# A two-layer fp32 block on one core: the first weight chunk computed by passes, the modulation passes and several loads moved to later places in the stream

## What is computed (the reference, cut)

```python
def reference(x, ..., w_in, ..., c_2, ctx_2, c_ctx_2, w_mod_2, ...):
    x = first_block(x, norm_in_g, w_in, ...)      # retention + gated linear recurrence
    return second_block(x, c_2, ctx_2, ...)       # two layers, with modulation

def first_block(x, ...):
    xn = rms_norm(x, norm_in_g)                   # x: 256 tokens x 1024
    proj = xn @ w_in                              # 1024 x 6144, all fp32
    q, k, v, g_ret, x_lru, g_lru = split(proj)
    q, k = rotary(q), rotary(k) * d ** -0.5       # 8 heads of 128
    y_ret = group_norm(retention(q, k, v)) * silu(g_ret)
    y_lru = rg_lru(causal_conv(x_lru), ...) * silu(g_lru)
    return rms_norm(x + concat(y_ret, y_lru) @ w_out, norm_out_g)

def second_block(x, c, ctx, c_ctx, ...):
    for l in range(2):
        mod = silu(c) @ w_mod[l] + b_mod[l]       # 1024 x 6144, one row each
        mod_c = silu(c_ctx) @ w_mod[l] + b_mod[l]
        ...                                       # mixing branches and FFN, modulated by mod, mod_c
```

## Time and profile before

| what | us |
|---|---|
| runs without a profile: median of 3 (lowest, highest) | 1670.08 (1669.75, 1671.25) |
| the profiled execution, its own time | 1669.85 |
| its span, first to last instruction | 1668.1 |
| around the span | 1.75 |
| PE / DVE / ACT busy in the span | 1655.0 / 1237.9 / 853.8 |

### The profile page before, as it was taken

How to read it: one execution, slowest core, us unless ns; L and a number is a source line. 1 busy time by engine, 2 the same in 40 slices (tenths; PEclk the granted TensorE clock), 3 DMA queues, 4 the chain that set the end, 5 groups by cost and what they waited for, 6 DMA issues and landing times.

```text
span 1668.1 us, 25166 instructions
## 1 busy us (share of the span) xinstructions
PE 1655.0 (99%) x9776; PEld 1421.6 (85%) x9776; DVE 1237.9 (74%) x2154; ACT 853.8 (51%) x1398; POOL 0.2 (0%) x4
## 2 busy tenths in 40 slices
PE   9999999999999999999999999999999999999998
PEld 9898888778887778889888888888778999989997
DVE  7999967966787897857887775347756776677874
ACT  7676655654344443356444442347553455576653
POOL 0000000000000000000000000000000000000000
PEclk9999999999999999999999999999999999999999
DMA  8657743132235345523555556224522354545553
GB/s 343 237 203 265 247 142 104 64 127 77 69 105 187 114 146 204 201 88 133 123 189 185 187 184 222 90 76 141 113 76 76 119 162 151 190 162 174 183 204 125
DMA packets 80230, 258.02 MB, mean 155 GB/s; under 512 B 14448, under 2 KB 18800, under 8 KB 79472
## 3 DMA queue, kind: packets, MB, share of 16 engines
q1 hardware_dynamic: 74352, 248.02, 45.6%
q10 hardware_dynamic: 5760, 8.39, 1.5%
HBM read 255.31 MB, written 1.07 MB: 154 GB/s over the span
## 4 chain that ended last, share of the span: by engine, by line
PE 87%; DVE 7%; ACT 3%; issue 2%; DMA 1%; ACTq 0%; SPq 0%; DVEq 0%
PE bank L796 73%; PE bank L960 3%; PE bank L1138 2%; PE bank L1154 2%; DVE w_lo L1996 2%; PE bank L1126 2%; PE bank L1234 2%; DMA w_raw<-in_weights 1%; ACT w_hi L1345 1%; PE bank L1220 1%; DVE mod_w L2052 1%; DVE junk_gate L2052 0%; DVE ptmp L2410 0%; DVE hT_lo L2421 0%; PE bank L911 0%
## 5 line engine op out<-in xcount | busy, mean ns | idle before, releaser
L1996 DVE TENSOR_TENSOR w_lo<-w_raw,w_hi 128x1024 fp32r<-128x1024 f32 (+1 forms) x356 | 428.0, 1210 | 252.6 <-ACT w_hi L1345 251.4
L1345 ACT ACTIVATE w_hi<-w_raw 128x1024 fp32r<-128x1024 f32 (+1 forms) x356 | 370.2, 1048 | 333.1 <-PE bank L796 280.3
L796 PE MATMUL bank<-hT_hi,w_hi 128*128 128x512 f32 (+1 forms) x1280 | 446.6, 349 | 0.0
L796 PE MATMUL bank<-hT_hi,w_lo 128*128 128x512 f32 (+1 forms) x1280 | 437.6, 342 | 0.0
L796 PE MATMUL bank<-hT_lo,w_hi 128*128 128x512 f32 (+1 forms) x1280 | 437.3, 342 | 0.0
L796 PEld LDWEIGHTS bank<-hT_hi,w_hi 128*128 128x128 f32 x1280 | 242.6, 190 | 28.2 <-issue 1.7
L796 PEld LDWEIGHTS bank<-hT_hi,w_lo 128*128 128x128 f32 x1280 | 242.5, 189 | 28.2
L796 PEld LDWEIGHTS bank<-hT_lo,w_hi 128*128 128x128 f32 x1280 | 242.8, 190 | 27.0 <-issue 1.0
L2052 DVE SCALAR_TENSOR_TENSOR mod_w<-mod_w,c_rows 128x1024 f32<-128x1024 f32 x102 | 124.3, 1218 | 8.5 <-DMA mod_w<-in_mod_weights 8.3
L796 PE MATMUL bank<-w_hi,hT_hi 128*128 128x512 f32 x272 | 114.4, 420 | 0.0
L796 PE MATMUL bank<-w_lo,hT_hi 128*128 128x512 f32 x272 | 106.7, 392 | 0.0
(11 more groups left out here) (408 smaller groups left out, 2704.4 us busy)
## 6 DMA issues: line engine op xcount, KB each, us to landing
w_raw<-in_weights SPq DMA_DIRECT2D x356, 512.0 KB, 4.4
mod_w<-in_mod_weights SPq DMA_DIRECT2D x102, 512.0 KB, 4.1
nbias<-in_window_bias ACTq DMA_DIRECT2D x32, 128.0 KB, 3.2
resid_c<-in_ctx ACTq DMA_DIRECT2D x2, 1024.0 KB, 5.3
gain_mix<-gain_rows SPq DMA_DIRECT2D x3, 512.0 KB, 5.7
gain_ffn<-gain_rows SPq DMA_DIRECT2D x3, 512.0 KB, 4.3
c_rows<-in_conditions SPq DMA_DIRECT2D x1, 1024.0 KB, 5.8
gatew<-in_gate_weights SPq DMA_DIRECT2D x1, 1024.0 KB, 11.5
```

Source lines behind the costliest of these rows:

```text
L796: mm = pe.matmul(held[key][:, oc], st, mv_, start=(opens and k == 0 and t == 0 and i == 0), stop=(closes and k == tiles - 1 and t == 2), s ...
L1345: a.activation(w_hi[:, p % RING, :, used], w_raw[:, p % RING, :].rearrange("p (k n) -> p k n", k=KP)[:, :, used], ACT.Copy).then_inc(hi_re ...
L1996: v.tensor_tensor(w_lo[:, p % RING, :, used], w_raw[:, p % RING, :].rearrange("p (k n) -> p k n", k=KP)[:, :, used], w_hi[:, p % RING, :, ...
```

## The change

The diff has six parts: PE computes the first chunk by passes, with the waits before each pass (`gemm_first`); DVE makes `xT_lo` of a group ahead of `w_lo`, where it was behind; one of the four scaling instructions goes from DVE to ACT; 24 warm-up matmuls become 22; the loads of the conditions, rotary tables, masks and gate weights go behind two to three more weight pieces; and the first two passes of modulation leave their early places in DVE's list, so that every later place takes the job before, with one pass more at two later places, and the loads of the jobs move accordingly.

```diff
-WARM = 24
+WARM = 22
 def mod_after():
-    at = [5, 6, 7, 9, 12, 15, 18, 21, 24, 27, 30, 34, 37, 40, 42, 44]
+    at = [8, 9, 10, 12, 15, 18, 21, 24, 27, 30, 34, 37, 39, 40, 42, 44]
     at += [51, 52, 54, 54, 56, 57]
@@ SP, in the loop over pieces p
-                if p == RING:
+                if p == RING + 2:
                     sp.dma_start(c_rows[:], c_in).then_inc(c_loaded, 16)
-                if p == RING + 2:
+                if p == 2 * RING + 1:
                     sp.dma_start(rot[:], rot_in).then_inc(rot_loaded, 16)
                     sp.dma_start(tab[:, P:NTAB], tab_in[:, P:NTAB]).then_inc(tab_loaded, 16)
-                if p == 2 * RING - 1:
+                if p == 2 * RING + 2:
                     sp.dma_start(gatew[:], gatew_in).then_inc(gatew_loaded, 16)
@@ PE
                 pe.wait_ge(*xn_ready.at(("b1", g // 2)))
+                if g == 0:
+                    pe.wait_ge(*xn_left.at(0))
+            def gemm_first(banks):
+                at, n = pieces[0], KD // KP
+                for p in range(n):
+                    s = (at + p) % RING
+                    pieces[0] = at + p + 1
+                    pe.wait_ge(hi_ready, at + p + 1)
+                    pe.wait_ge(*xT_hi_ready.at(p))
+                    for t, (w, x) in enumerate(((w_hi, xT_hi), (w_hi, xT_lo), (w_lo, xT_hi))):
+                        if t == 1:
+                            pe.wait_ge(*xT_ready.at(p))
+                        if t == 2:
+                            pe.wait_ge(lo_ready, at + p + 1)
+                        for key, subs in banks:
+                            ps = psum(key) if p or t else take(pe, key)
+                            for i, (oc, wc, xcols) in enumerate(subs):
+                                for kk in range(KP):
+                                    k = p * KP + kk
+                                    mm = pe.matmul(ps[:, oc], w[:, s, kk, wc], x[:, k, xcols], start=(k == 0 and t == 0 and i == 0),
+                                                   stop=(k == KD - 1 and t == 2), skip_group_check=True)
...
-            gemm_T(("in", 0), xs, xT_hi, xT_lo, inputs=xT_ready.at)
+            gemm_first(blocks_T(("in", 0), 4, None, xs))
@@ ACT
             a.activation(rs[:, 0:2], ss[:, 0:2], ACT.Sqrt, scale=1.0 / D, bias=eps[:]).then_inc(*A.tell(root_ready, "b1"))
+            act.wait_ge(*xn_inv.at(0))
+            a.activation(xn1[:, 1, 0:COLS], resid[1][:, 1, 0:COLS], ACT.Copy, scale=rs[:, 3:4]).then_inc(*A.tell(xn_left, 0))
...
-            split_hi(RING + 1)
-            act.wait_ge(c_loaded, 16)
-            a.activation(c_rows[:], c_rows[:], ACT.Silu).then_inc(*A.tell(c_ready, 0))
+            split_hi(RING + 2)
...
             lru_in(0)
+            split_hi(2 * RING)
+            act.wait_ge(c_loaded, 16)
+            a.activation(c_rows[:], c_rows[:], ACT.Silu).then_inc(*A.tell(c_ready, 0))
             lru_in(1)
@@ DVE
-            for half in range(2):
+            for half, t in ((0, 0), (1, 0), (1, 1)):
...
             for g in range(KD // 2):
-                split_lo(g + 1)
                 dve.wait_ge(*xT_hi_ready.at(g))
...
                 W.mark(xT_ready, g)
+                split_lo(g + 1)
...
-            split_lo(RING + 1)
-            dve.wait_ge(*c_ready.at(0))
-            mod_ops(1)
-            split_lo(6)
-            mod_ops(1)
+            split_lo(RING + 2)
             for i in range(2):
                 conv_pair(i)
                 split_lo(8 + i)
+            dve.wait_ge(*c_ready.at(0))
             mod_ops(1)
...
             ret_lo(2)
-            mod_ops(3)
+            mod_ops(4)
             split_lo(39)
...
             split_lo(42)
-            mod_ops(1)
+            mod_ops(2)
             split_lo(43)
```

More of the change, by code:

```diff
@@ L581, in build @@
     xn_ready = Counter("xn_ready")
+    xn_inv = Counter("xn_inv")
+    xn_left = Counter("xn_left")
     diag_ready = Counter("diag_ready")
@@ L597, in build @@
                qk_root, qk_ss, resid_ready, ret_hi, ret_inv, ret_rows, ret_root, ret_var, ret_y, root_ready, rows_ready, xT_hi_ready,
-               xT_ready, xn_ready, diag_ready, inv_ready, left_ready, right_ready, yT_hi_ready, yT_ready, gcol_ready, stat_ready, zo_ready, eps_ready)
+               xT_ready, xn_ready, xn_inv, xn_left, diag_ready, inv_ready, left_ready, right_ready, yT_hi_ready, yT_ready, gcol_ready, stat_ready, zo_ready, eps_ready)
     by_name = {c.name: c.sem for c in signals}
@@ L843, in _ @@
             xs = slice(0, T)
+            def gemm_first(banks):
[17 more added lines that the diff above has]
+                                                   stop=(k == KD - 1 and t == 2), skip_group_check=True)
+                            if t == 2 and key == banks[-1][0]:
+                                mm.then_inc(piece_used, 1)
+                                plan[("filled", key)] = ("piece", 0, at + n, at + n)
+                            elif t == 2 and p == n - 1:
+                                mm.then_inc(*filled(key))
+                                b, count = plan[("filled", key)][1:3]
+                                plan[("filled", key)] = ("bank", b, count, at + n)
             def gate(n):
@@ L2010, in _ @@
             dve.wait_ge(*root_ready.at("b1"))
-            v.reciprocal(rs[:, 2:4], rs[:, 0:2]).then_inc(*W.next())
+            v.reciprocal(rs[:, 2:4], rs[:, 0:2]).then_inc(*W.tell(xn_inv, 0))
             dve.wait_ge(*W.last())
-            for half in range(2):
+            for half, t in ((0, 0), (1, 0), (1, 1)):
                 cols = slice(half * COLS, (half + 1) * COLS)
-                for t in range(NT):
-                    v.tensor_scalar(xn1[:, t, cols], resid[1][:, t, cols], rs[:, 2 + t:3 + t], None, ALU.mult)\
-                        .then_inc(*(W.tell(xn_ready, ("b1", half)) if t == NT - 1 else W.next()))
+                v.tensor_scalar(xn1[:, t, cols], resid[1][:, t, cols], rs[:, 2 + t:3 + t], None, ALU.mult)\
+                    .then_inc(*(W.tell(xn_ready, ("b1", half)) if t == half else W.next()))
             for g in range(KD // 2):
-                split_lo(g + 1)
                 dve.wait_ge(*xT_hi_ready.at(g))
```

## The result

The changed kernel takes 1677.22 us (median of 6 runs, 1676.11 to 1678.78), the kernel before 1670.56 beside it (6 runs): a ratio of 1.0039 with a 95% interval of 1.0029 to 1.0049. It is slower, as forecast, but by 6.7 us, not 4.1, and 0.4 us beyond the top of the range. The profiled execution took 1677.38 us, with a span of 1675.6; that is 7.53 more than the one before, against the 4.14 of the prediction's sum.

The account below looks back on a forecast made before the run. TensorE, busy 1655.0 of 1668.1 us, bounds the kernel; from 122 to 223 delays of VectorE or piece 43's load count in full. 1669.85 - 1.72 + 5.86 = 1673.99, with 0.23 for the median 1674.2 us; range 1671.4 to 1676.8.

Parts of the forecast that it names:

- the last one: From piece 43 to 223 us: VectorE carries the chain, so its delay of 5.86 counts in full, not TensorE's 4.7.
- The loss at piece 43: SP's load of piece 43 waits behind job 14's load, goes out 9.1 later and lands 5.86 us later.
- the bound of 7.1: Upper bound of the loss at piece 43, if piece 40's late load adds up to 1.3 us.
- I take no such delay: Pieces 40 and 41: the late load of piece 40 was given no cost, though up to 1.3 us was possible.
- The head: Start to piece 12: first product at 10.26, 1.28 earlier; 1.72 us won in all, bounds 1.2 to 1.9.
- the 0.54 between pieces 7 and 12: TensorE's loss over these pieces, 14.94 instead of 14.40 us, forecast to go because VectorE's w_lo is ready earlier.
- so weights come earlier: Head's load queue: conditions, tables and gate weights go behind weights, so weights land earlier; priced at nothing.
- The clock rival: TensorE's wait at piece 43 drops its clock, losing 2.2 us more: 1676.4 us, chance 0.12.
- VectorE's private lead: Rival: VectorE keeps 2.6 us of its own lead until 127, so the loss is 3.3: 1671.7 us, chance 0.12.
- That only TensorE's idle time counts: Rival: VectorE makes good the rest before 223, leaving 4.7 - 1.7 = 3.0 us: 1673.1 us, chance 0.13.
- The loss at piece 43 was real: Against the rival of no loss there, the load being late from the full queue, not its issue: 1668.4 us, chance 0.08.
- The head does win: Against the rival that a new wait replaces the old one in the head: 1675.9 us, chance 0.08.

Follow-up runs that it names:

- e1: The changed kernel with the load of job 14 behind piece 44 instead of piece 42: 1672.84 us, ratio 1.0015.
- e4: The kernel before with one modulation pass moved from behind piece 38 to behind piece 42: 1675.96 us, ratio 1.0028.
- e7: The changed kernel with the context's load issued six entries earlier in ScalarE's list: 1675.15 us, ratio 1.0027.
- e9: e7 with the loads of jobs 12 and 13 behind piece 41 instead of pieces 39 and 40: 1674.52 us, ratio 1.0024.
- e2: The changed kernel with the loads of jobs 12 and 13 behind piece 41, those of 14 and 15 behind piece 45: 1671.83 us, ratio 1.0009.
- e5: e2 with the context's load issued six entries earlier in ScalarE's list: 1668.31 us, ratio 0.9985.
- e8: e5 with the first jobs' loads behind pieces 8, 11, 13, 14 and the gate weights' load at piece 12 instead of 10: 1668.09 us, ratio 0.9984.
- e6: The kernel before with the context's load issued six entries earlier in ScalarE's list: 1669.81 us, ratio 0.9993.
- e3: The kernel before with the head part of the diff alone; loads, conditions and passes stay where they were: 1671.91 us, ratio 1.0009.

## Why the prediction was right in its direction and short in its size

**The step that failed is the last one**, "VectorE carries the chain from there to 223, so what counts is not TensorE's 4.7 but the 5.86": a delay at piece 43 was taken to reach the end unchanged. VectorE's delay did reach piece 59 in full, but VectorE does not carry the chain all the way. In the chain of waits of the kernel before, then of the changed kernel, it leaves VectorE behind `w_lo` of piece 55 for the load of piece 59, and goes on over ScalarE's split of that piece and the statistics of the context:

```profile
182.80 1.15 DVE w_lo L1996
...
183.97 6.39 DMA w_raw<-in_weights
...
190.38 1.06 ACT w_hi L1345
191.45 1.04 ACT sg L1533 x2
```

```profile
188.02 1.15 DVE w_lo L2031
...
189.20 8.45 DMA w_raw<-in_weights
...
197.67 1.06 ACT w_hi L1377
198.73 1.05 ACT sg L1568 x2
```

This load goes out 5.23 later, which is VectorE's delay, and takes 2.06 longer: it lands 7.29 later, and by 7.29 `w_lo` of piece 58 is late, by 7.26 TensorE. In the five other traces with the context's load in its old place (e1 to e4 and a second one of the kernel before), the landing of piece 59 and `w_lo` of piece 58 are late by the same, to 0.02. In all seven the load of piece 59 takes 6.39 to 8.60 us; in the five kernels with the context's load issued early it takes 4.91 to 5.65, and TensorE does not wait there in any of them. The prediction gave this landing no price. Nor had the place room in the profile of before, though TensorE did not wait: its first matmul on `sg` starts 0.20 after the end of the activation that it needs, in the changed kernel, where it waited, 0.14; so 0.06 was left. And the landing is no property of the kernel: the second profile of the kernel before, taken beside e7 (one run, 1670.95 us, 1.1 above the first), has 7.6 for the context's load, 7.07 for piece 59, and this row on PE, with a lag of +1.05 behind it.

```profile
196.15 1.94 PE L898 MATMUL bank<-tab,sg 128*128 128x128 f32 x16 [0.81 <-ACT sg L1541]
```

In the changed kernel's trace this took 2.06 on the chain (1.7 on TensorE), in medians some 1.3 of the 2.6 us by which the forecast of 4.1 fell short of 6.7.

**The loss at piece 43 was mis-sized: 5.86 forecast, 6.60 in the trace** (5.23 and the lead of 1.37), inside the bound of 7.1. "I take no such delay, since one load less is queued ahead of that pair" was wrong: the load of piece 40 goes out at 128.77 and takes 6.5, `w_hi` and `w_lo` of pieces 40 and 41 follow late, and the pass that SP waits for starts 1.1 later than the sum had it (140.84 + 1.37 = 142.21 against 141.12). The shorter landing, 4.31 for 4.57, gave 0.26 back. e9 takes the late loads away and has 5.52; e7, with the late loads, has 7.41, so the size scatters by more than the 0.74 that were missing.

**The head was right at the start and short at piece 12.** 10.26 was forecast for the first product, 10.21 came. The scaling took 0.72 us on ScalarE in the wait that was to hide it, and `w_hi` of piece 0 started at 8.28 (8.29 before). But of the 0.54 between pieces 7 and 12 only some 0.1 came back: the lead went from 1.29 to 1.37, not to 1.72. The failed sentence is "so weights come earlier": the moved tables, masks, gate weights and first jobs now stand ahead of pieces 10 to 12, two of whose loads take 10.3 and 12.7 us. The other executions of this head lead by 0.83 to 1.93 behind piece 12 (e1, e2, e5, e7, e9), so 1.37 is itself one draw; the bounds of 1.2 to 1.9 were about right.

**The clock rival, given 0.12, did happen in part.** Behind the gap of 3.55 us TensorE's granted clock was 0.50, and the step from piece 43 to 44 took 4.28 instead of 2.83: 1.45 lost, not the 2.2 estimated. (That estimate took the lower level from the spacing of the warm-up matmuls; the clock column of the earlier trace rows reads 1.00 in both stretches.) The Trainium skill (TensorE: Matmul & The Clock Gate, What's actually happening) has an idle TensorE fall back to 1.2 GHz, and these rows agree. VectorE does not quite cover it: in e2, e4, e5 and e8, where the clock stayed at 1.00 there, TensorE's lag from piece 46 to 57 is 0.7 less than that of `w_lo` (in e4 2.66 against 3.35). So `w_lo`, 5.23 late at piece 43 and 5.22 at 50, would by itself have made TensorE some 4.5 late; it was 5.57 late, and about 1.0 of that is the clock's. In this execution it did not reach the end, because TensorE then waited 1.51 for ScalarE at piece 58. In e7, which has no such wait, the chain goes over TensorE from 145 to 205, and some 0.4 counted (5.59 against 5.86 - 0.69 = 5.17, an estimate). At pieces 57 to 58 in e2, where nothing covers it, the clock cost 1.6.

**The other rivals fell.** VectorE's private lead was not there (`w_lo` of 43 lost more than forecast, not less). The loss at piece 43 was real (e1). The head does win (e5 against e6: 1.5 us with the waits out of the way). That only TensorE's idle time counts would have given a smaller loss; it was larger. But what the prediction held against this rival, that the chain follows VectorE without a gap, is not so, as the rows of piece 59 show.

Put together, along the chain of the profiled execution: forecast +4.14; 0.35 less lead; 0.74 more at piece 43; 2.06 more at the load of piece 59, which makes 7.29. Measured were 7.53; the 0.24 left over came behind piece 63 or around the span, and no cause was found.

What the change could have been is e5 or e8: the same edits with the jobs' loads behind the pieces that they held up, and the context's load earlier, 1668.1 to 1668.3 us, 0.15% faster than the kernel before and 9 us faster than the change.

What stays open is why the context's load lands in 5.6 us in one execution and 7.6 in another of the same kernel, and in 8.8 and 9.2 in e3 and e2. The Trainium skill (DMA: Bandwidth & Descriptors, Queues, rings and completion order) says that SP's and ACT's queues run on the same 16 engines and take turns on them. That fits the weight loads that become slow beside it, 9.95 instead of 7.12 for piece 57; but in e1 and e4 the load of piece 57 takes 4.4 beside it, and both loads are there in every one of these kernels, so it does not say when they hurt each other.

## What to carry to other kernels

Where one list issues loads for two users, a wait for the one holds up the other: after moving work later, go through that list and look at what stands behind each wait that has now become real; a number in a list gave 4.4 us back. And a delay that is followed to the end through one profile crosses transfers whose landing is only that profile's: read the whole chain behind it row by row, ask of each load on it how its landing scatters, and give a loss there a price before calling the rest of the way neutral.

## What the runs showed of the hardware

- A 1 MB load on ACT's queue beside SP's weight loads landed in 5.6 to 9.2 us when issued behind the square root of head 7 (seven traces), and in 5.0 to 6.9 when issued some 7 us earlier in the list (five).
- The granted clock was at 0.50 behind 3.55 us without a matmul (152.50 to 155.20), and stayed at 1.00 behind the 1.51 at piece 58; in e2 it was at 0.50 behind 2.67 us, in e1 behind 2.00, and in e3 it stayed at 1.00 behind 2.07.
- A transfer's issue on SP, 0.33 us in most rows, took 1.56 us beside the context's load (the load of piece 57 at 184.07; 1.22 in the kernel before), but 0.43 in e1 and e4.
